# Attention trunk on one core: mask of the forgetting pairs, order of the last output groups, and three smaller moves

## The reference

```
A: stick-breaking   z = q.k/8, strictly causal
                    w = sigmoid(z) * prod over later keys of sigmoid(-z)
B: chunked softmax  QK-norm; own chunk of 64 and 8 chunks before; bias by clipped distance
C: forgetting       QK-norm; z = q.k/8 + cum[query] - cum[key], causal (key <= query); softmax
                    cum = cumulative sum of log_sigmoid(forget logit + b)
mixed = concat(oA * silu(gA), oB * silu(gB), oC * silu(gC));  out = x + mixed @ w_out
```

## Time and profile before

| | |
|---|---|
| runs | 1044.74, 1042.63, 1043.52 us |
| profiled execution, its own time | 1041.87 us |
| its span | 1040.1 us |
| mean granted clock of TensorE | 0.998 |
| busy: TensorE matmul / VectorE / ScalarE / GpSimd | 1009.0 / 683.7 / 631.0 / 102.8 us |

### The profile page before, as it was taken

How to read it: one execution, slowest core, us unless ns; L and a number is a source line. 1 busy time by engine, 2 the same in 40 slices (tenths; PEclk the granted TensorE clock), 3 DMA queues, 4 the chain that set the end, 5 groups by cost and what they waited for, 6 DMA issues and landing times.

```text
span 1040.1 us, 16138 instructions
## 1 busy us (share of the span) xinstructions
PE 1009.0 (97%) x5752; PEld 911.0 (88%) x5752; DVE 683.7 (66%) x1306; ACT 631.0 (61%) x1232; POOL 102.8 (10%) x90
## 2 busy tenths in 40 slices
PE   6999999999999999999999999999999998999998
PEld 6888989899899898998998998998998997787887
DVE  5656675765756756667667547879889787877200
ACT  6658775766766767767758658666567555543000
POOL 1210201101211011011011001002011010000000
PEclk9999999999999999999999999999999999999999
DMA  8244151431531513413414314304214228722921
GB/s 252 83 140 117 34 149 49 104 99 47 129 87 45 151 49 82 122 41 100 104 51 124 80 32 107 77 21 117 67 25 125 61 58 253 230 88 74 349 96 38
DMA packets 118064, 105.50 MB, mean 101 GB/s; under 512 B 10048, under 2 KB 94024, under 8 KB 117984
## 3 DMA queue, kind: packets, MB, share of 16 engines
q1 hardware_dynamic: 115904, 104.43, 36.0%
q10 hardware_dynamic: 2080, 0.04, 0.1%
HBM read 62.44 MB, written 19.98 MB: 79 GB/s over the span
## 4 chain that ended last, share of the span: by engine, by line
PE 75%; DVE 13%; ACT 5%; DMA 3%; issue 3%; SPq 1%; POOL 1%; ACTq 0%; DVEq 0%; POOLq 0%
PE psP L1223 36%; PE psO L1314 8%; PE psT L1296 7%; PE psS L1275 4%; PE psP L1227 4%; PE psS L1276 4%; PE psP L1362 3%; PE psS L1362 3%; DVE big L1005 2%; PE psO L1362 2%; DVE rb L1127 2%; PE psP L1332 2%; PE psT L1245 2%; DVE pt L1138 1%; DMA stack<-stack 1%
## 5 line engine op out<-in xcount | busy, mean ns | idle before, releaser
L1223 PE MATMUL psP<-big 128*128 128x384 f32 (+1 forms) x2304 | 476.9, 345 | 1.4 <-DVE big L1005 0.9
L1223 PEld LDWEIGHTS psP<-big 128*128 128x128 f32 x2304 | 395.3, 189 | 8.7 <-DVE big L1005 1.3
L1138 DVE TENSOR_TENSOR pt<-psT,pt 128x512 fp32r<-128x512 f32 (+1 forms) x224 | 143.1, 641 | 139.8 <-ACT pt L943 138.9
L943 ACT ACTIVATE pt<-psT 128x512 fp32r<-128x512 f32 (+1 forms) x224 | 125.1, 559 | 116.2 <-PE psT L1296 116.0
L1227 PE MATMUL psP<-big 128*128 128x512 f32 x576 | 156.6, 404 | 0.0
L1314 PE MATMUL psO<-pt,vst 128*128 128x512 f32 (+3 forms) x576 | 138.9, 340 | 7.4 <-DVE pt L1138 6.7
L1296 PE MATMUL psT<-identr,z 128*128 128x128 f32 x816 | 125.2, 272 | 0.0
L1227 PEld LDWEIGHTS psP<-big 128*128 128x128 f32 x576 | 102.3, 189 | 18.1
L1314 PEld LDWEIGHTS psO<-pt,vst 128*128 128x128 f32 x576 | 99.9, 188 | 19.9 <-issue 9.5
L1296 PEld LDWEIGHTS psT<-identr,z 128*128 128x128 f32 x816 | 102.2, 140 | 15.4
L1108 DVE CUSTOM_DVE_ANT_0 z<-psS,rb 128x640 f32<-128x640 f32 (+7 forms) x128 | 89.4, 699 | 37.1 <-PE psS L1276 18.7
(11 more groups left out here) (115 smaller groups left out, 1077.8 us busy)
## 6 DMA issues: line engine op xcount, KB each, us to landing
stack<-stack SPq DMA_DIRECT2D x192, 128.0 KB, 2.3
wraw<-in_w_in_dram SPq DMA_DIRECT2D x90, 192.0 KB, 2.6
wraw<-in_w_in_dram SPq DMA_DIRECT2D x24, 256.0 KB, 3.6
mixed_scratch<-mst SPq DMA_DIRECT2D x24, 256.0 KB, 2.3
mixed_scratch<-gate SPq DMA_DIRECT2D x24, 256.0 KB, 3.0
wraw<-in_w_out_dram SPq DMA_DIRECT2D x24, 256.0 KB, 3.6
rb<-decay_scratch SPq DMA_DIRECT2D x8, 512.0 KB, 4.1
big<-mixed_scratch SPq DMA_DIRECT2D x8, 512.0 KB, 5.8
```

The costliest lines, as they stand in the source:

```text
L943: nc.scalar.activation(pt[:, ci % PTR, 0, 0:w], psT[:, m % NT, 0:w], ACT.Copy).then_inc(s_hi, 1)
L1138: nc.vector.tensor_tensor(pt[:, ci % PTR, 1, 0:w], psT[:, m % NT, 0:w], pt[:, ci % PTR, 0, 0:w].bitcast(F32), ALU.subtract).then_inc(s_eva ...
L1223: ins = nc.tensor.matmul(dst[:, 0:TOKW - first], hT[a][:, k, i * P:(i + 1) * P], wpair[b][:, k, first:TOKW], start=(k == 0 and q == 0), st ...
```

## The change

In the forgetting group the mask matmul goes. GpSimd instead takes, for each block, the 128 bias columns of the block's own key tile and writes them with 1e30 at the shut places into one of two buffers `diag`; VectorE's bias step is split into a far part (all columns but the last 128, with `rb`) and a near part (with `diag`), the near one taking the far one's minimum as its start. `own` now lies in the same memory as `diag`, and is written at the first stick-breaking block. The constants for the mask go. Output groups 0 to 5 come one after another; 6 and 7 stay interleaved. The first residual is due at 0.3 instead of 1.7. From pair 4 on, the next pair's weights 2, 3 and 4 are due at 1.5, 1.9 and 2.3 instead of 1.1, 1.6 and 2.1 (the first turn step is due at 1.35).

```diff
@@ tables of due places, and the cost of a scores step
-        return total + (123 if group(n) == 2 else 0)
+        return sum(2 * max(109, w * 0.449) for _, _, w in score_parts(n)[1])
+AT = {'diag': -0.6, ...
+BEHIND_TURN = {('weights', 2): 1.5, ('weights', 3): 1.9, ('weights', 4): 2.3}
+RESIDUAL = [0.3, 7.7, 9.7]
-        found += [... for (kind, *rest), at in NEXT.items()
+        ahead = NEXT if j < PPG else {**NEXT, **BEHIND_TURN}
+        found += [... for (kind, *rest), at in ahead.items()
-        if r in (1, 7, 9):
-            found.append((0.7, ("residual", r // 4)))
+        found += [(at % 1, ("residual", c)) for c, at in enumerate(RESIDUAL) if at // 1 == r]
-    order = [(MF * (i // 2) + k + STAGGER * (i % 2) + 0.7 * (i // 2), i, k) for i in range(len(FIRST)) for k in range(MF)]
+    order = [(MF * min(i, 6) + k + STAGGER * (i == 7), i, k) for i in range(len(FIRST)) for k in range(MF)]
+            if group(n) == 2:
+                timed.append((n + AT["diag"], ("diag", n)))
@@ GpSimd: each of its steps waits for the one before it in PLAN, diag steps among them
+                if kind == "diag":
+                    n = step[1]
+                    s, b = n // TT % 2, n % TT
+                    pool.wait_ge(s_bias[s], 16 * bias_loads(n))
+                    pool.wait_ge(s_z, n - 1)
+                    nc.gpsimd.affine_select(out=diag[:, n % 2, :], in_=rb[:, s, b * P:(b + 1) * P], compare_op=ALU.is_gt,
+                                            fill=BIG, base=1, pattern=[[-1, P]], channel_multiplier=1).then_inc(s_diag, 1)
@@ ScalarE and GpSimd, start
-                    nc.scalar.activation(identb[:, :], ident_raw, ACT.Copy)
-                    nc.scalar.activation(mask[:, :], mask_raw, ACT.Copy).then_inc(s_identr, 1)
-            nc.gpsimd.memset(mask_raw, 0.0).then_inc(s_const, 1)
-            nc.gpsimd.affine_select(out=mask_raw, in_=mask_raw, ...
@@ VectorE
-                    nc.vector.memset(own[:, 0:SEQ - P], 0.0)                                  (step constants)
-                    nc.vector.tensor_copy(own[:, SEQ - P:SEQ], ident).then_inc(s_own, 1)
+                    (both, at the first stick-breaking block, i == 0)
-                    add = rb[:, s, 0:w] if group(n) == 2 else rb[:, s, P * WIN - w:P * WIN]
+                    low = 3.0e38
+                    if group(n) == 2:
+                        add = diag[:, n % 2, :]
+                        if w > P:
+                            nc.vector.tensor_tensor_reduce(out=z[:, at:at + w - P], in0=psS[:, off:off + w - P],
+                                                           in1=rb[:, s, 0:w - P], scale=1.0, scalar=low, op0=ALU.add,
+                                                           op1=ALU.min, accum_out=small[:, q, 1:2]).then_inc(s_far, 1)
+                            far = n - FIRST_DIAG + 1
+                            dve.wait_ge(s_far, far - -(-far // TT))
+                            at, off, w, low = at + w - P, off + w - P, P, small[:, q, 1:2]
+                        dve.wait_ge(s_diag, n - FIRST_DIAG + 1)
+                    else:
+                        add = rb[:, s, P * WIN - w:P * WIN]
                     nc.vector.tensor_tensor_reduce(out=z[:, at:at + w], in0=psS[:, off:off + w], in1=add, scale=1.0,
-                                                   scalar=3.0e38, op0=ALU.add, op1=ALU.min,
+                                                   scalar=low, op0=ALU.add, op1=ALU.min,
@@ TensorE, scores
-                        if masked:
-                            end = off + P * (b + 1)
-                            ins = nc.tensor.matmul(psS[:, end - P:end], identb[:, :], mask[:, 0:P],
-                                                   start=False, stop=True)
```

More of the change, by code:

```diff
@@ L41 @@
 NSOFT = NORMED * 16
+FIRST_DIAG = PPG * 16
 FW = HG
@@ L172, in extras @@
     if j + 1 < PAIRS:
-        found += [(at % 1, (kind, j + 1, *rest)) for (kind, *rest), at in NEXT.items()
+        ahead = NEXT if j < PPG else {**NEXT, **BEHIND_TURN}
+        found += [(at % 1, (kind, j + 1, *rest)) for (kind, *rest), at in ahead.items()
                   if at // 1 == r and (kind != "sq" or j + 1 < NORMED)]
@@ L340 @@
     _t += turns_of(_s)
-POOL_KIND = [s for s in PLAN if s[0] in ("square", "sq", "gatew") or (s[0] == "norm" and s[1] >= NORMED and s[3] == 0)]
+POOL_KIND = [s for s in PLAN if s[0] in ("square", "sq", "gatew") or s[0] == "diag"
+             or (s[0] == "norm" and s[1] >= NORMED and s[3] == 0)]
 POOL_BEHIND = {}
-_n = {"square": 0, "sq": 0, "norm": 0, "gatew": 0}
+_n = {"square": 0, "sq": 0, "norm": 0, "gatew": 0, "diag": 0}
 for _i, _s in enumerate(POOL_KIND):
-    POOL_BEHIND[_s] = (POOL_KIND[_i - 1][0], _n[POOL_KIND[_i - 1][0]]) if _i else ("const", 6)
+    POOL_BEHIND[_s] = (POOL_KIND[_i - 1][0], _n[POOL_KIND[_i - 1][0]]) if _i else ("const", 4)
     _n[_s[0]] += 2 if _s[0] == "sq" else 1
@@ L432, in build @@
         ident = identr[:, :].bitcast(F32)
-        identb = sb("identb", [P, P], BF16)
-        mask = sb("mask", [P, P], BF16)
-        own = sb("own", [P, SEQ], U8)
+        diag = sb("diag", [P, 2, P])
+        own = diag[:, :, :].rearrange("p a b -> p (a b)").bitcast(U8)
         small = sb("small", [P, 8, 4])
@@ L978, in _ @@
                 if kind == "constants":
-                    dve.wait_ge(s_identr, 1)
-                    nc.vector.memset(own[:, 0:SEQ - P], 0.0)
-                    nc.vector.tensor_copy(own[:, SEQ - P:SEQ], ident).then_inc(s_own, 1)
                     nc.vector.memset(gain[0:HD, 0:1], -HD ** -0.5)
@@ L1123, in _ @@
                     if i == 0:
+                        dve.wait_ge(s_identr, 1)
+                        nc.vector.memset(own[:, 0:SEQ - P], 0.0)
+                        nc.vector.tensor_copy(own[:, SEQ - P:SEQ], ident).then_inc(s_own, 1)
                         dve.wait_ge(s_own, 1)
@@ L1266, in _ @@
                         pe.wait_ge(s_sig, held - NSOFT)
-                    if n == 16 * PPG:
-                        pe.wait_ge(s_identr, 2)
                     qs = stack[:, s, 0, b * P:(b + 1) * P]
-                    off, parts = score_parts(n)
-                    for pi, (col, key, w) in enumerate(parts):
+                    _, parts = score_parts(n)
+                    for col, key, w in parts:
                         dst = psS[:, col:col + w]
-                        last = pi == len(parts) - 1
-                        masked = group(n) == 2 and last
                         nc.tensor.matmul(dst, qs, stack[:, s, 1, key:key + w], start=True, stop=False)
-                        ins = nc.tensor.matmul(dst, qs, stack[:, s, 2, key:key + w], start=False, stop=not masked)
-                        if masked:
-                            end = off + P * (b + 1)
-                            ins = nc.tensor.matmul(psS[:, end - P:end], identb[:, :], mask[:, 0:P],
-                                                   start=False, stop=True)
+                        ins = nc.tensor.matmul(dst, qs, stack[:, s, 2, key:key + w], start=False, stop=True)
                     ins.then_inc(s_scores, 1)
```

19 lines of the change are left out of this document (6 added, 13 removed).

## The result

The changed kernel took 1036.82 us, median of 6 runs (1033.93 to 1039.79), beside 1043.34 for the kernel before on the same chip (6 runs, 1042.55 to 1044.74). The ratio is 0.9936, 95% interval 0.9921 to 0.9952. It is faster by 6.5 us; 11.6 were forecast. The profiled execution took 1036.77 us, with a span of 1035.0; the two spans differ by 5.1.

What follows compares the result with a forecast made beforehand. Forgetting pairs were taken as bound by TensorE's sum of work. Terms: masks -7.7, forgetting additions +4.1, stick-breaking -1.2, start -0.4, own places +0.5, last pair -6.9: -11.6, so 1031.9 us against the runs' median 1043.52; range 1026.0 to 1038.5.

Steps and rivals of the forecast that it cites:

- rival D: Forgetting pairs: a mask costs only its own step, so removal gives 2.6 us instead of 7.7; total 1037.0; 5%.
- the two holds: Forgetting pairs: VectorE waits for selects behind GpSimd's powers, 1.1 late at block 1, 1.8 at block 11; net 2.2 + 0.9.
- What is late next: the second turn ... Nothing: Moved weights 2 to 4: second turn's values come over 1 us later, loads stay ahead of use; no cost.
- The split: Forgetting pairs: dividing VectorE's bias step costs 0.25 us a block, reaching TensorE only mid-pair, 1.0 us in all.
- Almost covered: 3 x 0.3 = 0.9: Block 11 of three forgetting pairs: near part 1.8 us late, but next turn nearly in time; 0.9 us more.
- A: Forgetting pairs: every delay of VectorE's queue reaches TensorE, 23.8 us added instead of 4.1; total 1051.6; 4%.
- B: Forgetting pairs: holds at blocks 1 and 11 pass in full, 10.8 us added instead of 4.1; total 1038.6; 10%.
- E: Forgetting pairs: VectorE's free time swallows all additions and moved weights show, -1.8 us instead of 4.1; total 1026.0; 10%.
- Rival C: Last pair gives little: group 0 waits 3.0 us for weights 6 and 7, clock falls again; total 1036.8; 14%.
- Own places at block 128: Memset and cast moved to the first stick-breaking block, before first scan and turn: 0.5 us more (0 to 1.1).
- (2): Last pair: earlier first residual brings weights 7 forward by up to 2.7 us, leaving a wait of 0.6.
- (4): Last pair: TensorE comes earlier into the last unit, whose scans bound it; 0.3 us given back.

Runs made afterwards that it cites:

- e4: Kernel before without its 64 mask matmuls, nothing in their place (changes the output), planner's block cost lowered: 1034.95 us, ratio 0.992.
- e9: Changed kernel with selects ahead of GpSimd's powers and weights 2 to 4 moved only in the stick-breaking pairs: 1031.94 us, ratio 0.9875.
- e10: Changed kernel with selects ahead of GpSimd's powers and, of weights 2 to 4, only weights 2 moved: 1030.45 us, ratio 0.987.
- e1: Changed kernel with GpSimd's selects due at n - 0.9 instead of n - 0.6, ahead of its powers: 1032.0 us, ratio 0.9889.
- e5: Changed kernel with output groups interleaved again as before, first residual still at 0.3: 1041.22 us, ratio 0.9976.
- e6: Changed kernel with the first residual back at 1.7, output groups still in a row: 1039.14 us, ratio 0.9944.
- e12: The changed kernel again without edit, on the third chip: 1035.64 us, ratio 0.992 to the kernel before.
- e8: Kernel before with groups in a row, first residual sooner and weights moved, but mask matmuls kept, no split or selects: 1039.35 us, ratio 0.995.
- e2: Changed kernel with weights 2, 3 and 4 back at 1.1, 1.6 and 2.1: 1039.12 us, ratio 0.9954.
- e7: e1 with weights 4 also put behind the key copies, at 2.45 instead of 2.3: 1035.16 us, ratio 0.991.
- e11: Changed kernel with selects ahead of GpSimd's powers only at block 1 of each forgetting pair: 1032.51 us, ratio 0.9881.

## Why the prediction was right in direction and 5 us too large

**Masks: right.** 7.7 forecast. Taking them away alone gives 8.4 by the medians and 6.8 in the forgetting stretch (e4); the forecast's 0.12 each lies between 0.11 and 0.13. The 0.04 of rival D is excluded. So is the estimate of 3.6 us by the isolated gap that the Trainium skill gives ("TensorE: Matmul & The Clock Gate", section Back-to-back issue gap).

**What the forgetting pairs add: here a step failed.** The forecast was 4.1 us. Measured: 297.3 before, 6.8 less without masks, so 290.5, and 298.2 after: 7.7 added. The kernels of e9, e10 and e1 lead from one to the other, each a step of the change further. The forecast column has the prediction's terms taken apart: the two holds in full, 4 x 1.1 + 0.9, and the 2.2 that it took off the first for the moved weights.

| forgetting pairs, us | stretch | step | forecast |
|---|---|---|---|
| before, without masks (e4) | 290.5 | | |
| split, and selects ahead of the powers (e9) | 292.4 | +1.9 | +1.0 |
| weights 2 moved as well (e10) | 289.8 | -2.6 | -2.2 |
| weights 3 and 4 moved as well (e1) | 292.9 | +3.1 | 0 |
| selects behind the powers (after) | 298.2 | +5.3 | +5.3 |
| sum | | +7.7 | +4.1 |

Each stretch is one trace. Four traces with the same code in these pairs (after, e5, e6, e12) lie between 297.5 and 298.6, so a step is good to about 1 us.
- *"What is late next: the second turn ... Nothing"* (weights 3 and 4) is the step that failed: 3.1 us instead of nothing. It looked at VectorE's queue and at the age of the loads, but not at what leaves SP right behind them: the copies of the keys, for which TensorE waits 1.0 to 1.3 us at block 4 in three of the four pairs of e8, and 2.0 us in all in e1. With weights 2 the whole move was to gain 2.2 and costs 0.5 (e1 against e9). What it costs depends on what stands around it: 1.3 in the changed kernel (after against e2), 2.7 where the masks are kept (e8 against before).
- The split, *"4 x 0.25 = 1.0"*, was too small and at the wrong place. In the middle of a pair, where the forecast had it, nothing shows: TensorE's weight load there stands 0.36 to 0.37 us before, after and in e1 alike. It shows at the first values wait, 0.9 instead of 0.63 (e9 against e4), and in pair 4 at the keys.
- The holds came out at their full size, 5.3. At block 1 the hold passes nearly in full, 3 to 4 of 4.4, but by a path that was not named: the norms were counted as queued behind it without asking who waits for them. TensorE does, for its transposes, 0.70 in each of four pairs, at a place where it had not stood before. Block 11, *"Almost covered: 3 x 0.3 = 0.9"*, fits within what the runs can tell: 0.35 in the trace after, 0 to 1.5 by the runs. (Its working adds up to 383.5, not 383.6, and so to 1.7 late; nothing hangs on it.)

Of the rivals, A is excluded (23.8). B has the right path for block 1 but not for block 11, and its 10.8 is about as far above 7.7 as the forecast's 4.1 is below. E is excluded: 7.7 were added, nothing gained. Rival C's 1036.8 is just what was measured, and by luck: its wait of 3.0 us for the weights was 1.29, the clock did not fall, and the last pair gave 5.2 where C had 2.0.

**Stick-breaking pairs: right.** 1.2 forecast for pairs 9 and 10, and the wait there went from 0.76 to 0.24, not 0.15. Own places at block 128: the cast took 0.17 us, not the 0.82 of the earlier trace rows, so its price of 1.1 was nearer 0.4, and the stretch came out at -1.1 instead of -0.7; e12 has -0.2 against the same trace, so the sum is less sure than the waits. At the start 0.2 came of the 0.4, in part because the scaling of gains took over the cast's long time; the traces of kernels with this same start lie between 55.2 and 56.7, so neither figure is clear of noise.

**Last pair: 5.2 of 6.9.** The groups in a row are worth 3.4 (e5 against after, last pair) and do what was said: no wait over 1 us for mixF, none for banks. (2) was mis-sized: an earlier residual was to bring weights 7 forward by 2.7 us, and it stood at 874.54 (L1030, 873.85 + 0.69) instead of 875.5, 1.0 sooner, so the wait for it is 1.29, not 0.6. Putting the residual back makes this wait 0.7 longer and the stretch no longer (e6). And (4) was mis-sized: the turn behind a 2.02 us scan costs 1.78, where 0.3 was forecast. The granted clock stayed at 1.00 in the profiled execution, as said.

**The spread.** The runs after spread over 5.9 us, those before over 2.2 here but over 6.0 to 7.6 on the three chips of the experiments, so the change did not bring the spread. The traces show one cause. Here is e10 in its last pair, by stretch, columns as in the earlier trace rows, and the wait that falls in it:

```profile
880.00:884.00 4.00, 1.74 (x8) 1.07 (x6) 3.97 (x5) 1.02 (x2) 0.00 (x0) 0.99 0.92 263
884.00:886.00 2.00, 1.83 (x6) 1.69 (x7) 1.82 (x4) 1.20 (x4) 0.00 (x0) 0.50 1.06 317
886.00:888.00 2.00, 2.00 (x7) 1.56 (x6) 1.97 (x2) 0.47 (x1) 0.00 (x0) 0.66 1.15 314
```

```profile
884.17 0.80 PE L1325 MATMUL psO<-pt,vst 128*128 128x256 f32 x2 [2.44 <-DVE pt L1157]
```

The same wait in the kernel after, 1.78 us, left the clock alone:

```profile
892.00:894.00 2.00, 1.64 (x9) 1.47 (x10) 1.44 (x3) 1.17 (x4) 0.00 (x0) 1.00 1.07 323
```

After 2.44 idle microseconds the clock granted was 0.50, the lower level (1.2 GHz), and 0.66 in the next stretch: by these rows 2 x 0.50 + 2 x 0.34, or 1.7 us of full speed lost. Of the six runs after, the two with a mean clock of 0.998 took 1039.79 and 1039.17, the other four, at 1.000, 1033.93 to 1036.87: some 3 us, which would be the lost clock and a longer wait in front of it. Of the 6.5 us measured, this makes one or two uncertain. Which place it was in those two runs is not known, since only one execution of a kernel has a trace. Whether moving the scan would avoid it was not tried.

**Left open.** How the 0 to 1.5 us of block 11 divide; by what path weights 3 and 4 delay the copies beyond the load in front of them; why the clock falls after some waits and not after others of the same length; and how far e10's lead over e1 goes, whose ratios come from different chips (0.987 and 0.9889, intervals that just overlap).

## What to carry to other kernels

When a step is moved, list what is queued behind it on every engine it touches, the DMA queue too, and for each of these ask who waits for it: here the lateness on VectorE was forecast to 0.1 us, and the unforeseen cost came from the key copies behind the moved weights. When a helper engine takes over part of a step, place its instruction ahead of that engine's long jobs: moving the select by 0.3 of a block gave 5 us, almost as much as the whole change. A wait that is shortened below some place's neighbour moves on to the neighbour (e2, e7, e9), so compare the sum of a stretch, not the wait.

## What the runs showed of the hardware

- A 128-column bias step with a minimum that starts from another instruction's result takes 351 ns, one that starts from a constant 292 (56 and 8 times).
- The cast of 128 x 128 to bytes took 818 ns at 28.0 us in the kernel before and 165 ns at 633.95 after. A scaling of 64 x 2 at the first place took 0.16 us behind that cast, and 0.76 where it came first. GpSimd was at work beside both long ones; no run takes that away.
- TensorE's granted clock fell to 0.50 after waits of 1.80 us (e9, last pair), 1.84 (e11, first chunked pair), 1.97 (e6, last pair), 2.09 (e7, last pair), 2.44 (e10), 2.45 (e4, last pair), 2.57 (e6) and 2.79 (e9), both in the first chunked pair, and 3.78 before. It did not after 1.78 (after), 1.86 and 2.14 (e5, last pair), 2.04 (e10, first chunked pair), 2.09 (e8, last pair) and 2.14 (e11, block 4 of pair 4). So between 1.8 and 2.2 us the length of the wait alone does not tell. In e6, behind the 2.57:

```profile
72.00:74.00 2.00, 0.00 (x0) 0.00 (x0) 0.50 (x1) 1.15 (x3) 0.00 (x0) 0.97 0.72 150
74.00:76.00 2.00, 1.83 (x6) 1.83 (x7) 0.28 (x2) 0.68 (x2) 0.38 (x1) 0.50 0.99 281
```

In e9 behind the 1.80 (ended at 888.57), and in e8 behind the 2.09 (ended at 895.12):

```profile
889.00:893.00 4.00, 4.00 (x13) 3.15 (x12) 2.50 (x3) 1.56 (x4) 0.00 (x0) 0.57 1.10 317
```

```profile
895.00:897.00 2.00, 1.88 (x10) 1.66 (x11) 1.56 (x4) 1.53 (x4) 0.00 (x0) 1.00 1.12 328
```
